# Attention pairs of a one-core transformer block: the order of masks, decay tiles, a tap and weight loads

## The reference, cut to what matters

```python
p_l = h_lat @ w_in                     # input projection, context too
qc, kc, vc, lic, lfc = _mlstm_inputs(...)   # q and k: depthwise conv of 5 taps, then silu
h = _bidir_mlstm(...)                  # gated linear recurrence, both directions
a_l = _banded_attention(qa_l, ka_l, va_l, ka_c, va_c, sink)   # softmax in a band of 128, and the context
y_l = jnp.concatenate([m_l, a_l], -1) @ w_out
```

## Time and profile before

| what | value |
|---|---|
| median of 3 runs (lowest to highest) | 2130.13 us (2129.56 to 2136.0) |
| span of the profiled execution | 2127.8 us |
| PE busy in the span | 2091.4 us, 98% |
| DVE, ACT, POOL busy | 72%, 43%, 9% |
| share of the chain that ended last: PE, DVE, DMA, ACT | 86%, 4%, 3%, 2% |

### The profile page before, as it was taken

The page is one execution under the profiler, slowest core; times in us unless marked ns, Lnnn a source line. Parts: engine busy times, 40 slices in busy tenths (PEclk is TensorE's granted clock), DMA queues, the critical chain, the costliest instruction groups (busy, mean ns, idle before and its releaser), DMA issues.

```text
span 2127.8 us, 31643 instructions
## 1 busy us (share of the span) xinstructions
PE 2091.4 (98%) x11508; PEld 1768.0 (83%) x11510; DVE 1527.0 (72%) x2520; ACT 905.6 (43%) x1631; POOL 192.8 (9%) x212
## 2 busy tenths in 40 slices
PE   8999999999999999999999999999999999999998
PEld 4888888888888888899878878877888888888886
DVE  5778888777648878675665465866867777767787
ACT  4622222222237446542565555734532323336445
POOL 0000000000000001090111002821000000000001
PEclk9999999999999999999999999999999999999999
DMA  8144444555459664733231002732244434349773
GB/s 298 33 142 147 149 134 129 160 167 159 129 186 348 193 215 148 209 101 117 74 108 41 21 21 66 182 109 99 75 134 140 136 104 153 123 139 341 257 234 112
DMA packets 261841, 310.38 MB, mean 146 GB/s; under 512 B 19350, under 2 KB 164686, under 8 KB 261710
## 3 DMA queue, kind: packets, MB, share of 16 engines
q1 hardware_dynamic: 261422, 308.52, 45.4%
q10 hardware_dynamic: 288, 0.13, 0.0%
HBM read 242.13 MB, written 66.45 MB: 145 GB/s over the span
## 4 chain that ended last, share of the span: by engine, by line
PE 86%; DVE 4%; DMA 3%; ACT 2%; issue 1%; POOL 1%; SPq 1%; DVEq 0%; POOLq 0%; ACTq 0%
PE psum L1327 11%; PE psum L1328 11%; PE psum L1329 11%; PE psum L1527 6%; PE psum L1529 6%; PE psum L1528 6%; PE psum L2056 3%; PE psum L2058 3%; PE psum L2057 3%; PE psum L1347 2%; PE psum L1346 2%; PE psum L1345 2%; PE psum L3078 2%; PE psum L875 2%; PE psum L876 2%; PE psum L877 2%
## 5 line engine op out<-in xcount | busy, mean ns | idle before, releaser
L1327 PE MATMUL psum<-x_mix_h,x_op_h 128*128 128x512 f32 x640 | 251.2, 393 | 1.3 <-DVE v_sum L1135 1.2
L1328 PE MATMUL psum<-x_mix_l,x_op_h 128*128 128x512 f32 x640 | 249.8, 390 | 0.0
L1329 PE MATMUL psum<-x_mix_h,x_op_l 128*128 128x512 f32 x640 | 249.5, 390 | 0.0
L1527 PE MATMUL psum<-s_high 128*128 128x512 f32 x616 | 240.0, 390 | 0.3 <-DVE s_low L1514 0.3
L1528 PE MATMUL psum<-s_low,s_high 128*128 128x512 f32 x616 | 239.9, 389 | 0.0
L1529 PE MATMUL psum<-s_high,s_low 128*128 128x512 f32 x616 | 239.9, 389 | 0.0
L1514 DVE TENSOR_TENSOR s_low<-s_raw,s_high 128x1024 fp32r<-128x1024 f32 x154 | 186.9, 1217 | 50.5 <-ACT s_high L1475 50.5
L1475 ACT ACTIVATE s_high<-s_raw 128x1024 fp32r<-128x1024 f32 x154 | 161.3, 1057 | 124.1 <-PE psum L1529 56.3
L1019 ACT ACTIVATE x_op_h<-raw 128x512 fp32r<-128x512 f32 x140 | 86.1, 627 | 203.6 <-PE psum L1329 121.1
L1019 ACT ACTIVATE x_op_h<-w_sum 128x512 fp32r<-128x512 f32 x160 | 97.1, 625 | 162.9 <-DVE w_sum L997 107.1
L1327 PEld LDWEIGHTS psum<-x_mix_h,x_op_h 128*128 128x128 f32 x640 | 120.4, 188 | 25.4 <-issue 1.8
(11 more groups left out here) (408 smaller groups left out, 5069.6 us busy)
## 6 DMA issues: line engine op xcount, KB each, us to landing
raw<-in_ffn_w SPq DMA_DIRECT2D x88, 512.0 KB, 5.4
f_terms<-g_half SPq DMA_DIRECT2D x154, 256.0 KB, 2.3
s_raw<-f_terms SPq DMA_DIRECT2D x154, 256.0 KB, 3.2
s_raw<-in_ffn_w SPq DMA_DIRECT2D x154, 256.0 KB, 4.0
ada_slice<-in_w_ada SPq DMA_DIRECT2D x112, 256.0 KB, 3.1
c_raw<-in_ffn_w SPq DMA_DIRECT2D x22, 512.0 KB, 3.5
p_raw<-in_w_in SPq DMA_DIRECT2D x22, 512.0 KB, 4.0
early<-in_w_ada SPq DMA_DIRECT2D x16, 512.0 KB, 6.6
```

What stands on the lines that cost most here:

```text
L1327: nc.tensor.matmul(o, wh[:, k], high(k), start=i < 4 and k == 0, stop=False, skip_group_check=i > 3)
L1328: nc.tensor.matmul(o, wh[:, k], low(k), start=False, stop=False, skip_group_check=i > 3)
L1329: last = nc.tensor.matmul(o, wl[:, k], high(k), start=False, stop=k == KH - 1, skip_group_check=i > 3)
L1527: nc.tensor.matmul(o, h[:, 0, rows], h[:, 1], start=i == 0 and q in (0, 1, 6), stop=False, skip_group_check=True)
```

## The change

Five edits. SP: the loads at the first k group no longer stand ahead of tile 0's store, and all five pairs of loads are issued behind the decay rows of the pair in which ACT makes the high part that frees their slots (`HIGH_IN`). POOL: a piece's low part is made by four instructions of 2 x 128 columns instead of one, with one semaphore increment at the last; unit 6's low parts come behind mask 2 instead of mask 1, and unit 7's behind mask 9 instead of mask 8. ACT: the second decay tile of a pair is done ahead of the first taps of that pair; and behind the last pair the first tap of group 79 is done ahead of the silus 1 to 3 of k.

```diff
@@ proj_sp
-            pieces_after, pairs_passed = [], 0
+            pieces_due, pairs_passed = {}, 0
...
                 while j > PRE and pairs_passed < begins_in(j):
                     decay_pair_sp(sp, pairs_passed)
+                    for q in pieces_due.pop(pairs_passed, ()):
+                        piece_load(sp, q)
                     pairs_passed += 1
-                    for q in pieces_after:
-                        piece_load(sp, q)
-                    pieces_after = []
                 if j in PREPARED_AT:
                     pieces = [2 * PREPARED_AT[j] + 2, 2 * PREPARED_AT[j] + 3]
-                    if j > PRE:
-                        pieces_after = pieces
+                    if j >= PRE:
+                        pieces_due[HIGH_IN[PREPARED_AT[j]]] = pieces
...
+            for pieces in pieces_due.values():
+                for q in pieces:
+                    piece_load(sp, q)
@@ proj_low_pool
-                nc.gpsimd.tensor_tensor(low[:, :, cols], p_raw[:, q % 2], high[:, :, cols].bitcast(F32),
-                                        ALU.subtract).then_inc(p_lo, 1)
+                for k in range(0, KD, 2):
+                    last = nc.gpsimd.tensor_tensor(low[:, k:k + 2, cols], p_raw[:, q % 2, k:k + 2],
+                                                   high[:, k:k + 2, cols].bitcast(F32), ALU.subtract)
+                last.then_inc(p_lo, 1)
@@ mixed_act
+                for i in decays[1:]:
+                    decay_tile_act(act, i)
                 if p + 2 == ATT_PAIRS:
                     silu_k_act(act, range(1))
                 for j in groups_done(p):
                     group_act(act, j)
-                for i in decays[1:]:
-                    decay_tile_act(act, i)
+            done = groups_done(ATT_PAIRS - 1)
             keep_pair_act(act, ATT_PAIRS - 1)
-            silu_k_act(act, range(1, 3))
+            group_act(act, done[0])
+            silu_k_act(act, range(1, 2))
             pair_rows_act(act, ATT_PAIRS - 1)
-            silu_k_act(act, range(3, 4))
-            done = groups_done(ATT_PAIRS - 1)
-            for j in done[:-1]:
+            silu_k_act(act, range(2, 4))
+            for j in done[1:-1]:
                 group_act(act, j)
@@ mixed_pool
-            LOW_AT = {2: POOL_LOW[0],
-                      decays_in(next(p for p in range(ATT_PAIRS) if first_of(6) in groups_done(p))).stop: POOL_LOW[1]}
+            LOW_AT = {decays_in(1).stop: POOL_LOW[0], decays_in(HIGH_IN[POOL_LOW[1]]).stop: POOL_LOW[1]}
```

## The result

The changed kernel took 2116.67 us (median of six runs, 2115.36 to 2121.69), the kernel before 2129.43 us on the same chip (six runs, 2127.29 to 2136.0): a ratio of 0.9943 with a 95% interval of 0.9931 to 0.9954, or 9.8 to 14.7 us. The span fell from 2127.8 to 2115.3 us.

What follows compares the result with a forecast made beforehand. PE was taken to set the pace where attention pairs and input projection share it, so removed stops shorten the run: 5.71 + 0.50 + 1.45 + 1.99 + 1.7 = 11.35 us off 2130.13, giving 2118.8 us, range 2115 to 2124.

Steps and rivals of the forecast that it cites:

- Part 1: SP's decay stores and GpSimd's masks come earlier, so PE's stops of 1.50, 3.19 and 1.02 us go: 5.71 us gained.
- mask 10 takes over: Rival: GpSimd's low parts run longer, mask 10 comes at 1099.2, pair 8's exponentials wait; 3.2 us back, 2122.0; chance 0.09.
- a decay chain that falls behind: Rival: SP's in-order store, landing and load take 7.2 us a tile and PE waits; 2138.4 us; chance 0.03.
- Part 2: ACT's second decay tile ahead of the tap: the 0.50 us stop at 1084.92 goes; loss from later taps taken as 0.
- Part 3: GpSimd's low parts by 256 columns: DVE's scalings wait less, two stops of 0.50 go and 0.45 of a third; 1.45 us.
- DVE is shut out until the last quarter: Rival: GpSimd's queued quarters go ahead of DVE's scalings, and the three stops grow by 1.2 us each; 2124.8 us; chance 0.06.
- Part 4: ACT's last tap first: PE's 1.99 us stop before the last projection group goes, and the low clock behind it, 1.7 us.
- the reordering frees more: Rival: stops too short for the profile's rows and a second low clock go too; 2117 us; chance 0.06.
- the clock falls anyway: Rival: the granted clock falls at the end of the stretch regardless, or behind another short stop; 2120.5 us; chance 0.14.

Runs made afterwards that it cites:

- experiment 3: Kernel before with one edit each: SP's new order alone 2128.65 us, GpSimd's new mask order alone 2131.88 us, last tap ahead of silus alone 2126.62 us.

## Why the prediction was right

**Part 1, SP and the masks: right, step by step.** Every time of its chain came out within 2.3 us, and pair 0 itself started 1.07 us earlier: the store of tile 0 (1034.26 for "near 1035"), that of tile 1 (1045.44 for 1047.7), mask 3, mask 10, 4.2 us from the store of tile 2 to that of tile 3 (forecast 4.0 to 5.3). All three stops went. The rival that mask 10 takes over and the slower one, a decay chain that falls behind, are out: after the change no decay tile of ACT at pairs 6 and 7 waits for its mask. What the prediction didn't say is which order each stop belongs to. The 1.50 before pair 3 go with SP's order alone and stay gone with the masks undone. The 3.19 before pair 7 need both: with SP's order alone they stay, with the masks' alone they move to pair 8 (experiment 3). For the 1.02 before pair 9 the runs don't separate the two.

**Part 2, the tile ahead of the tap: right, taken 0 in a bound of 0 to 5.1.** The loss is there, 0.21 us from pair 4 to 5, of which 0.13 is a gap ahead of the scores at 1064.54. The tile's place is only part of it: with the tile back pair 4 keeps 0.10 of the loss, and with SP's order back it keeps none (8.60 us, as before). The cover named, DVE's waits for PE, stayed whole.

**Part 3, low parts by 256 columns: right in kind, mis-sized.** Two scalings were to lose 0.85 us and lost 0.82 + 0.84 - 2 x 0.55 = 0.56 ahead of pair 13, so both stops of 0.50 went. The third stop, of which a third was to stay, went wholly: 0.24 us more. DVE's timeline ahead of pair 26 shows why. There the scaling took 1.89 us before, not 2.75, so 1.34 us lost made a stop of 0.69: a slack of 0.65. The 0.85 of the forecast would have left 0.20; the 0.41 lost after (0.67 and 0.84 us) left nothing, and the 1.20 lost with 512 columns left 0.55, which is the stop that was measured. The rival that DVE is shut out until the last quarter is out. The Trainium skill ("SBUF — State Buffer", section "Who interferes with whom") has the loser block for the whole instruction. The traces agree for the instruction that runs, 2.75, 1.28 and 0.84 us by its size; read as applying to quarters that are only queued, the rule fails.

**Part 4, the tail: right in this pair of executions, with one term that is a draw.** DVE's chain took 3.11 us (forecast 3.1). The stop went, and the low clock with it: 3.87 us measured for 1.99 + 1.7. But two other executions of the kernel before had no low clock there, so what the edit surely gives is the stop: the tail alone has a stretch of 277.49 us, 2.09 under the 279.58 of those two, which like it had the low clock behind pair 7; from pair 31 on the gain is 2.28 (16.03 us in those two, 13.75 with the tail alone). So the stop costs 2.28, and the low clock is the other 1.59 of the 3.87. In those two the fall came behind pair 7 instead and cost 1.6 us from pair 7 to 8, which the sum didn't have, since its profile showed a clock of 1.00 there; the full change takes that stop away as well. Against those two, the stretch after is 279.58 - 268.03 = 11.55 us shorter. That this is close to the 11.35 of the sum is luck: those executions have neither the 1.02 before pair 9 nor the low clock at the end, both of which the sum counts.

**Against the first profile the sum was 1.47 us short, and the term that was mis-sized is the price of a stop.** I took a stop at its idle time. Rows of matmuls overlap: in the timeline after, they start every 0.12 us and last 0.28, with ends that the profile models (1139.65, 1139.77, 1139.89). So the last row ahead of a stop reaches 0.16 us past the start that the next one would have had, and by this reading a stop costs about that much more than the idle time beside it. The starts of the pairs show it: 1.67 for 1.50, 0.65 for 0.50, 0.84 for 0.69, 1.13 for 1.02, and 3.91 for 3.69 with two stops. That makes 0.95 us for the seven stops of the pairs; 0.24 come from the third scaling, 0.18 at the end (the stop 0.29 over its idle time, the clock 0.11 under its 1.7), 0.31 from the pairs right behind the stops, less the 0.21 of part 2. Those 0.31 belong to the stops too: with 1024 columns, where the stops before pairs 13, 19 and 26 are back, pairs 13, 19 and 26 are 0.05 to 0.06 us longer again. What makes these pairs longer was not taken apart. The rest of the 2.1 us by which the forecast was high is the base: the six runs of before that this comparison used have a median 0.7 us under the 2130.13 of the first three. The rival that the reordering frees more, at 2117, thus came nearest by its number, but hardly by its reasons: the low clock in the stage behind stayed, and nothing became shorter except at the named stops and in the pair behind each. The rival that the clock falls anyway is out for this execution.

**Left open.** What varies outside the stretch from one execution to the next was not taken apart. Low parts by 128 columns, and the two stops of 0.27 and 0.35 in pairs 0 and 1, were not tried. No kernel that was run beats the full change by more than its runs spread.

## What to carry to other kernels

Where two in-order queues feed each other, look at both before moving anything on one: here the weight loads waited for low parts and the decay stores behind them, the masks' order alone only moved the long stop to the next pair, and SP's alone left it where it was. Long instructions of GpSimd that nobody waits for can still be cut, since DVE gets in between the pieces. And price a stop of PE by how far the next starts move, with the clock behind it as a term that may or may not fall due.

## What was not expected of the hardware

The granted clock fell behind the same stop in some executions and not in others. Behind the stop of 3.2 us before pair 7 it stayed at 1.00 in the first profile of before, was low for about 3.4 us in both others and with the tail alone, and for about 6.9 us with SP's order alone (0.57 over 8 us). Before pair 8 it fell for as long with SP's order back (a stop of 4.45 us) and with the masks alone (3.10 us), and before pair 7 for some 3.4 us with the masks back (3.97 us). Behind the stop of 2.0 us at the end it fell in the first profile of before, with the tail back and with the masks alone, and stayed at 1.00 in the other two of before and with SP alone. A fall cost 1.6 us, or 2.7 to 3.0 where it lasted twice as long, nearly as much as the stop itself. No stop under 1.9 us in this stretch had a low clock behind it in any profile of this study. What decides it between equal stops, the runs don't show.
